# A 31-tap depthwise convolution on TensorE, laid out as two token phases of 64 channels

## What is computed

```python
ga, gg = jnp.split(glu, 2, axis=-1)              # 512 tokens x 512 channels each
u = ga * jax.nn.sigmoid(gg)
u = causal_dwconv(u, conv_b_w, conv_b_b)         # 31 taps, one filter for each channel
b_out = jax.nn.silu(layernorm(u, ln_b_g, ln_b_b))
x = x + jnp.concatenate([a_out, b_out], axis=-1) @ w_out
```

## Time and profile before

| | |
|---|---|
| times of three runs | 2129.69, 2136.82, 2138.82 us; median 2136.82 |
| profiled execution | 2137.5 us: its span, and nothing is shown outside it |
| busy over the span | PE 92%, PEld 75%, DVE 51%, ACT 34%, POOL 49% |
| stage under change (sparse attention) | 204.5 to 318 us |
| matmuls of the convolution | 62 x 3 = 186, with 186 weight loads |

### The profile page before, as it was taken

The page is one execution under the profiler, slowest core; times in us unless marked ns, Lnnn a source line. Parts: engine busy times, 40 slices in busy tenths (PEclk is TensorE's granted clock), DMA queues, the critical chain, the costliest instruction groups (busy, mean ns, idle before and its releaser), DMA issues.

```text
span 2137.5 us, 31171 instructions
## 1 busy us (share of the span) xinstructions
PE 1975.8 (92%) x10443; PEld 1607.7 (75%) x10443; DVE 1098.4 (51%) x1811; ACT 733.2 (34%) x1233; POOL 1046.9 (49%) x576
## 2 busy tenths in 40 slices
PE   7888888979999999778999999999997799999997
PEld 5677666768887888556778888887876678888886
DVE  6777973654677696689333223132128834132232
ACT  4323234344222313435432222233226643222223
POOL 5466426535865644680554444456443244444442
PEclk9999999999999999989999999999999999999999
DMA  4224002323332333100333333334345423333332
GB/s 144 72 86 121 11 15 75 89 50 89 98 98 83 94 99 91 57 2 0 89 91 97 97 100 89 98 97 100 98 114 123 104 69 90 97 98 98 98 89 89
DMA packets 344697, 181.64 MB, mean 85 GB/s; under 512 B 28206, under 2 KB 335782, under 8 KB 344614
## 3 DMA queue, kind: packets, MB, share of 16 engines
q1 hardware_dynamic: 343872, 179.91, 30.1%
q10 hardware_dynamic: 742, 0.68, 0.1%
HBM read 162.73 MB, written 2.10 MB: 77 GB/s over the span
## 4 chain that ended last, share of the span: by engine, by line
PE 51%; issue 13%; DVE 11%; POOL 9%; POOLq 6%; DVEq 4%; ACT 4%; DMA 2%; SPq 0%; ACTq 0%
PE ACC L1464 16%; PE ACC L1465 15%; PE ACC L1470 15%; POOL WL L1128 7%; POOLq L1138 2%; DVE CV L2161 2%; DVE PTL L2261 1%; DVEq L2255 1%; POOLq L1311 1%; POOLq L1323 1%; ACT WH L565 1%; DVEq L2165 1%; DVE NMX L2249 1%; PE O L1586 1%; DVEq L2700 1%
## 5 line engine op out<-in xcount | busy, mean ns | idle before, releaser
L1128 POOL TENSOR_TENSOR WL<-RAW,WH 128x1024 fp32r<-128x1024 f32 (+1 forms) x308 | 733.0, 2382 | 785.2 <-ACT WH L565 717.8
L1464 PE MATMUL ACC<-PH,WH 128*128 128x512 f32 x1248 | 495.8, 397 | 11.9 <-DVE PL L1995 3.6
L1465 PE MATMUL ACC<-PL,WH 128*128 128x512 f32 x1248 | 489.9, 393 | 0.0
L565 ACT ACTIVATE WH<-RAW 128x1024 fp32r<-128x1024 f32 (+1 forms) x308 | 317.6, 1033 | 498.6 <-PE ACC L1470 415.5
L1464 PE MATMUL ACC<-QH,WH 128*128 128x512 f32 (+1 forms) x1136 | 431.1, 384 | 23.1 <-ACT WH L565 17.2
L1465 PE MATMUL ACC<-QL,WH 128*128 128x512 f32 (+1 forms) x1136 | 426.3, 380 | 0.0
L1470 PE MATMUL ACC<-PH,WL 128*128 128x512 f32 x1248 | 311.1, 391 | 0.0
L1464 PEld LDWEIGHTS ACC<-PH,WH 128*128 128x128 f32 x1248 | 236.9, 190 | 71.1 <-DVE PL L1995 4.8
L1470 PE MATMUL ACC<-QH,WL 128*128 128x512 f32 (+1 forms) x1136 | 271.9, 380 | 11.0 <-POOL WL L1128 10.8
L1465 PEld LDWEIGHTS ACC<-PL,WH 128*128 128x128 f32 x1248 | 236.7, 190 | 49.4 <-issue 1.0
L1470 PEld LDWEIGHTS ACC<-PH,WL 128*128 128x128 f32 x1248 | 234.0, 188 | 52.6 <-issue 3.3
(11 more groups left out here) (413 smaller groups left out, 2423.3 us busy)
## 6 DMA issues: line engine op xcount, KB each, us to landing
RAW<-in_mlp_w_dram SPq DMA_DIRECT2D x128, 512.0 KB, 4.1
RAW<-in_w_gate_dram SPq DMA_DIRECT2D x22, 512.0 KB, 3.8
RAW<-in_w_up_dram SPq DMA_DIRECT2D x22, 512.0 KB, 3.7
RAW<-in_w_in_dram SPq DMA_DIRECT2D x16, 512.0 KB, 3.9
RAW<-in_w_down_dram SPq DMA_DIRECT2D x16, 512.0 KB, 4.1
RAW<-in_ssm_w_glu_dram SPq DMA_DIRECT2D x16, 512.0 KB, 3.9
RAW<-in_w_kvf_dram SPq DMA_DIRECT2D x16, 512.0 KB, 3.9
RAW<-in_w_k_cross_dram SPq DMA_DIRECT2D x8, 512.0 KB, 4.1
```

The costliest lines, as they stand in the source:

```text
L565: act.activation(WH[:, s, 0:kc], RAW[:, s, 0:kc], ACT.Copy).then_inc(w_hi, 1)
L1128: pool.tensor_tensor(WL[:, s, 0:kc], RAW[:, s, 0:kc], WH[:, s, 0:kc], ALU.subtract).then_inc(w_lo, 1)
L1464: pe.matmul(ACC[s][:, 0:n], WH[:, s, k, :], xh[:, k, :], start=(k == 0), stop=False)
L1465: pe.matmul(ACC[s][:, 0:n], WH[:, s, k, :], xl[:, k, :], start=False, stop=False)
```

## The change

The 128 channels of a block are treated as two groups g of 64. For a group the partitions 0 to 63 hold the odd tokens and 64 to 127 the even tokens, 256 columns, behind 16 columns of zeros. One 128x128 matrix then carries up to four taps (from either phase to either phase), and a group takes 16 steps of three matmuls with 256 columns: 2 blocks x 2 groups x 16 x 3 = 192 matmuls. The two groups use the two halves of `ST`. For this:

- ScalarE issues four transfers that swap the halves of the tap weights and of the bias (`WSW`, `BSW`) where it rounded the taps before, and arranges and rounds the taps later (`phase_taps`: four small copies, a drain, the rounding), ahead of `rounded(3)`. `WC`, `WCH`, `WCL` are 128 columns wide in place of 124.
- between `memk` and `memv` it makes the phase layout `UP` of each block by four copies of 64x256 with a stride of two tokens, then a drain, and rounds 128x512 in place of 128x542.
- `convolved` is four copies of 64x256 that write every second token.
- GpSimd clears `WC` at the start, makes `EYE2` (two identities of 64 side by side, 128x64), clears the 16 columns ahead of `UH` and `UL`, and multiplies 16 x 64 in place of 8 x 128 columns for a set of matrices.
- the taps are spread over the tiles by the same rule, now 32 steps for a block in place of 31.
- some semaphores are merged (`f_exp`, `f_ln` into `f_soft`; `silu_done` into `branch_hi`) and unused ones dropped; no instruction is added or moved by it.

```diff
+LEAD = 16
+STEPS = 2 * LEAD
...
+        UP = at("UP", [P, 2, 2, T // 2], F32, 147968)
+        UH = at("UH", [P, 2, 2, LEAD + T // 2], F32R, 16384)
+        UL = at("UL", [P, 2, 2, LEAD + T // 2], F32R, 20736)
...
             act.wait_ge(vec_c, 2)
-            act.activation(WCH[:], WC, ACT.Copy).then_inc(wc_hi, 1)
+            bias = COLUMN["conv_b_b"][1]
+            for to, of in ((LOWER, UPPER), (UPPER, LOWER)):
+                act.dma_start(WSW[to, :], VEC[of, 1, 0:BCH * CONVW]).then_inc(vec_in, 16)
+                act.dma_start(BSW[to, :], VEC[of, 0, bias:bias + BCH]).then_inc(vec_in, 16)
+
+            def phase_taps():
+
+                act.wait_ge(vec_in, 16 * (len(VECTORS) + 3))
+                act.wait_ge(u_zero, 1)
+                for g, own_taps, swapped in ((0, LOWER, UPPER), (1, UPPER, LOWER)):
+                    for rows, taps in ((own_taps, VEC[own_taps, 1, 0:BCH * CONVW]), (swapped, WSW[swapped, :])):
+                        late = 1 if rows == UPPER else 0
+                        act.activation(WC[rows, :, g, late:late + CONVW],
+                                       taps.rearrange("p (k c) -> p c k", c=BCH)[:, 2:4, :], ACT.Copy)
+                act.drain()
+                act.activation(WCH[:], WC[:], ACT.Copy).then_inc(wc_hi, 1)
...
             act.activation(MD[:], MV[:], ACT.Sqrt).then_inc(mem_std, 1)
+            phase_taps()
             rounded(3)
...
                 if name == "memk":
+                    act.wait_ge(rope_done, 8)
                     for j in range(2):
                         act.wait_ge(u_ready, 3 + j)
-                        act.activation(UH[:, j, :], U[:, 2 + j, :], ACT.Copy).then_inc(u_hi, 1)
+                        for g, of in enumerate((LOWER, UPPER)):
+                            tokens = U[of, 2 + j, PAD:PAD + T].rearrange("p (m r) -> p r m", r=2)
+                            for r, to in ((1, LOWER), (0, UPPER)):
+                                act.activation(UP[to, j, g, :], tokens[:, r, :], ACT.Copy)
+                        act.drain()
+                        act.activation(UH[:, j, :, LEAD:], UP[:, j], ACT.Copy).then_inc(u_hi, 1)
...
                 act.wait_ge(diag_used, 4 * j + 4)
-                act.activation(CV[2 + j][:], ST[:], ACT.Identity, bias=column("conv_b_b", 2 + j))\
-                   .then_inc(conv_pe, 1)
+                for g, to in enumerate((LOWER, UPPER)):
+                    tokens = CV[2 + j][to, :].rearrange("p (m q) -> p q m", q=2)
+                    for q, of in ((1, LOWER), (0, UPPER)):
+                        bias = column("conv_b_b", 2 + j)[of] if of == to else BSW[of, 2 + j:3 + j]
+                        ins = act.activation(tokens[:, q, :], ST[of, g * T // 2:(g + 1) * T // 2], ACT.Identity, bias=bias)
+                ins.then_inc(conv_pe, 1)
...
+            pool.memset(WC[:], 0.0)
+            pool.drain()
...
-            pool.tensor_tensor(WCL[:], WC, WCH[:], ALU.subtract)
+            pool.tensor_tensor(WCL[:], WC[:], WCH[:], ALU.subtract)
+            pool.tensor_tensor(EYE2[:], IDENT[:, LOWER], IDENT[:, UPPER], ALU.add)
...
             def inputs_low(j):
+                if j == 0:
+                    for x in (UH, UL):
+                        pool.memset(x[:].bitcast(F32)[:, :, :, 0:LEAD], 0.0)
+                    pool.drain()
                 pool.wait_ge(u_hi, j + 1)
-                pool.tensor_tensor(UL[:, j, :], U[:, 2 + j, :], UH[:, j, :], ALU.subtract).then_inc(u_lo, 1)
+                pool.tensor_tensor(UL[:, j, :, LEAD:], UP[:, j], UH[:, j, :, LEAD:], ALU.subtract).then_inc(u_lo, 1)
...
-                    x = slice(k, k + T)
-                    mm = three(ST[:], DGH[j % 2][:, k % TAPS, :], DGL[j % 2][:, k % TAPS, :], UH[:, c, x], UL[:, c, x],
-                               k == 0, k == CONVW - 1)
+                    x = slice(1 + k, 1 + k + T // 2)
+                    mm = three(ST[:, g * T // 2:(g + 1) * T // 2], DGH[j % 2][:, k % TAPS, :], DGL[j % 2][:, k % TAPS, :],
+                               UH[:, c, g, x], UL[:, c, g, x], k == 0, k == LEAD - 1)
```

More of the change, by code:

```diff
@@ L199, in build_program @@
         CV = [at(f"CV{c}", [P, T], F32, (184320, 152576, 34816, 36864)[c]) for c in range(BCH)]
-        UH = at("UH", [P, 2, PAD + T], F32R, 16384)
-        UL = at("UL", [P, 2, PAD + T], F32R, 20736)
+        UP = at("UP", [P, 2, 2, T // 2], F32, 147968)
+        UH = at("UH", [P, 2, 2, LEAD + T // 2], F32R, 16384)
+        UL = at("UL", [P, 2, 2, LEAD + T // 2], F32R, 20736)
         DGH = [at(f"DGH{b}", [P, TAPS, P], F32R, (57344, 73728)[b]) for b in range(2)]
         DGL = [at(f"DGL{b}", [P, TAPS, P], F32R, (61440, 77824)[b]) for b in range(2)]
-        WCH = at("WCH", [P, BCH * CONVW], F32R, 210176)
-        WCL = at("WCL", [P, BCH * CONVW], F32R, 210688)
-        WC = VEC[:, 1, 0:BCH * CONVW]
+        WCH = at("WCH", [P, 2, 2, 2 * LEAD], F32R, 210176)
+        WCL = at("WCL", [P, 2, 2, 2 * LEAD], F32R, 210688)
+        WC = at("WC", [P, 2, 2, 2 * LEAD], F32, 211456)
+        EYE2 = at("EYE2", [P, 64], F32, 211968)
+        WSW = at("WSW", [P, BCH * CONVW], F32, 212224)
+        BSW = at("BSW", [P, BCH], F32, 212736)
+        LOWER, UPPER = slice(0, 64), slice(64, P)
         G = at("G", [P, 2 + T], F32, 155648)
@@ L358, in build_program @@
         rho_used, powers, w_made, c_made, cleared = (sem(n) for n in ("rho_used", "powers", "w_made", "c_made", "cleared"))
-        normed_x, un_ready, uc_ready = sem("normed_x"), sem("un_ready"), sem("uc_ready")
+        un_ready, uc_ready = sem("un_ready"), sem("uc_ready")
         glu_out = sem("glu_out")
         sq2_ready, sq2_used, diag2, bc2 = (sem(n) for n in ("sq2_ready", "sq2_used", "diag2", "bc2"))
-        fw_zero, fw_in, fw_hi, fw_lo, f_mm, f_abs, f_exp, f_ln, f_sum, f_ready = (
-            sem(n) for n in ("fw_zero", "fw_in", "fw_hi", "fw_lo", "f_mm", "f_abs", "f_exp", "f_ln", "f_sum", "f_ready"))
+        fw_zero, fw_in, fw_hi, fw_lo, f_mm, f_abs, f_soft, f_sum, f_ready = (
+            sem(n) for n in ("fw_zero", "fw_in", "fw_hi", "fw_lo", "f_mm", "f_abs", "f_soft", "f_sum", "f_ready"))
         split_hi, split_lo, stacked, bias_in = (
@@ L1072, in _ @@
             act.wait_ge(f_abs, 1)
[L1073 to L1075 removed]
+            act.activation(F[:], F[:], ACT.Exp, scale=-1.0).then_inc(f_soft, 1)
+            act.wait_ge(f_soft, 1)
+            act.activation(F[:], F[:], ACT.Ln, bias=ONES[:, 0:1]).then_inc(f_soft, 1)
             def split_high(c):
@@ L1149, in _ @@
             pool.wait_ge(wc_hi, 1)
-            pool.tensor_tensor(WCL[:], WC, WCH[:], ALU.subtract)
+            pool.tensor_tensor(WCL[:], WC[:], WCH[:], ALU.subtract)
+            pool.tensor_tensor(EYE2[:], IDENT[:, LOWER], IDENT[:, UPPER], ALU.add)
             pool.drain()
             def diagonals(j):
-                c, first = 2 + j // 4, j % 4 * TAPS
-                n = min(TAPS, CONVW - first)
+                c, g, half = j // 4, j // 2 % 2, j % 2
+                n = 2 * TAPS
                 if j >= 2:
@@ L1159, in diagonals @@
                 for to, w in ((DGH, WCH), (DGL, WCL)):
-                    taps = w[:].rearrange("p (k c) -> p k c", c=BCH)[:, first:first + n, c]
-                    ins = pool.tensor_tensor(to[j % 2][:, 0:n, :], IDENT[:, None, :].to_broadcast([P, n, P]),
-                                             taps.bitcast(F32)[:, :, None].to_broadcast([P, n, P]), ALU.mult)
+                    taps = w[:, c, g, half * n:half * n + n]
+                    ins = pool.tensor_tensor(to[j % 2][:].rearrange("p e (q f) -> p (e q) f", q=2),
+                                             EYE2[:, None, :].to_broadcast([P, n, 64]),
+                                             taps.bitcast(F32)[:, :, None].to_broadcast([P, n, 64]), ALU.mult)
                 ins.then_inc(diag_ready, 1)
@@ L1701, in convolve @@
                 for m in range(first, last):
-                    c, k = divmod(m, CONVW)
-                    j = 4 * c + k // TAPS
+                    c, k = divmod(m, STEPS)
+                    g, k = divmod(k, LEAD)
+                    j = 4 * c + 2 * g + k // TAPS
                     if k % TAPS == 0:
                         pe.wait_ge(diag_ready, j + 1)
-                    if k == 0 and c:
+                    if k == 0 and g == 0 and c:
                         pe.wait_ge(conv_pe, c)
-                    x = slice(k, k + T)
-                    mm = three(ST[:], DGH[j % 2][:, k % TAPS, :], DGL[j % 2][:, k % TAPS, :], UH[:, c, x], UL[:, c, x],
-                               k == 0, k == CONVW - 1)
-                    if k % TAPS == TAPS - 1 or k == CONVW - 1:
+                    x = slice(1 + k, 1 + k + T // 2)
+                    mm = three(ST[:, g * T // 2:(g + 1) * T // 2], DGH[j % 2][:, k % TAPS, :], DGL[j % 2][:, k % TAPS, :],
+                               UH[:, c, g, x], UL[:, c, g, x], k == 0, k == LEAD - 1)
+                    if k % TAPS == TAPS - 1:
                         mm.then_inc(diag_used, 1)
```

(6 more changed lines are left out.)

18 lines of the change are left out of this document (7 added, 11 removed).

## The result

| | median of the runs | lowest to highest | profiled span |
|---|---|---|---|
| before | 2135.19 us (20 runs) | 2129.69 to 2141.07 | 2137.5 |
| after | 2138.89 us (20 runs) | 2135.10 to 2142.89 | 2139.4 |

The account below looks back on a forecast made before the run. VectorE was taken to bound the sparse attention, the only stage with the convolution. TensorE -2.0, copies +1.9, start +0.5 and accumulator copies +0.2 sum to +0.6: 2138.1 on the span, 2137.4 beside the median, range 2130.5 to 2145.

Parts of the forecast that it names:

- TensorE's part, -2.0: Sparse attention: shorter products cut VectorE's three waits for ScalarE's rounded tile from 2.4 to about 0.4 us; range 0 to -3.4.
- VectorE's pace, as forecast: Sparse attention: VectorE, not TensorE, sets the pace; it stays as busy, and TensorE waits more for it in each tile.
- The rival of stalls that shift: Sparse stage: GpSimd's matrices slow VectorE's taps at other moments; a third less of 11 us excess gives 2133.5; chance 0.10.
- The copies, +1.9: Between `memk` and `memv`: ScalarE's eight copies delay the second `memv` rounding, so attention starts 1.9 us later.
- that chain has nothing spare: From the late `memv` rounding through GpSimd's remainders and SyncE's loads to the first score matmul: the delay passes on whole.
- The start, +0.5: Kernel start: ScalarE's four transfers delay the rounding of block 1 that TensorE wants, 0.5 us; ends 0 and +1.2.
- the thin cover of the square root: Kernel start: square root some 1.5 us late, its result wanted only after TensorE's sixteen matmuls; prices the +1.2 end.
- ScalarE's second set of copies, +0.2: Tile 23: four copies out of the accumulator in place of one hold up ScalarE's next exponential; +0.2 us, 0 to 0.8.
- Dear copies: Between `memk` and `memv`: strided copies cost 4.5 us in place of 1.9, giving 2140.0, or 2142.5; chance 0.10.
- The clock: Sparse stage: idler TensorE drops to half clock; six two-tile stretches and the channel sum give 2152; chance 0.08.
- 256 columns not faster: Convolution products: a weight load of 0.19 us sets the pace, so little comes back and the time is 2139; chance 0.04.
- The signs that were named: Profile after: expected product steps, waits, rounding, load and first-score times; stage clock under 0.9 or lower mean tap would refute.

Follow-up runs that it names:

- before + copies: Kernel before plus the eight copies and two drains between `memk` and `memv`, their result unused: 2137.27 us, ratio 1.0015.
- before + transfers: Kernel before plus the four transfers that swap the tap weights and bias at the start, their result unused: 2135.91 us, ratio 1.0002.
- before, 256 columns: Kernel before with its 186 convolution matmuls cut to the first 256 columns, nothing else changed: 2132.99 us, ratio 0.9992.
- after, moved: Kernel after with ScalarE's transfers put behind block 3's rounding, first copies ahead of `memk`'s end, second behind the first `memv` block: 2136.25 us, ratio 1.0009.
- the kernel before with early taps: Kernel before with 13 in place of 8 of VectorE's taps done ahead of the sparse stage: 2134.93 us, ratio 1.0008.
- the first group of experiments: Kernel before with 256 columns, copies or transfers, and kernel after with ScalarE's work moved: 2132.99, 2137.27, 2135.91, 2136.25 us.
- a stage with VectorE relieved: Block 1 of the convolution left out from tap 8 on (23 VectorE taps), in kernel before and kernel after: 2120.59 and 2122.57 us.

## Why the prediction was right, and which terms were off

The moments that the profiles of the kernels that compute everything show, in us. The stage is from the start of VectorE's first reduction to the end of its last tap; the third column is the way from the first tap to that reduction.

| kernel | first tap at | first tap to first reduction | stage |
|---|---|---|---|
| before | 169.05 | 36.0 | 86.3 |
| before + copies | 168.01 | 38.4 | 84.9 |
| before + transfers | 170.44 | 36.4 | 84.7 |
| before, 256 columns | 168.50 | 36.2 | 83.5 |
| after | 169.83 | 37.8 | 85.3 |
| after, moved | 169.74 | 35.8 | 85.0 |

(The line with 256 columns leaves half of each product out, as its expectation says.)

**TensorE's part, -2.0: the term that was mis-sized.** The three kernels whose stage is that of before have 86.3, 84.9 and 84.7 us. The profile that the prediction rested on shows the longest, with 2.4 us of waits for the rounded tile at 250 us; the other two have these waits too:

```profile
DVE PTL L2269 <- ACT PTH L720: 1.0, 2, 0.8
```
```profile
DVE PTL L2268 <- ACT PTH L719: 0.9, 2, 0.7
```

The term took the gain from one execution's stretch at half clock. In that stretch it had tile 12 right (1.9 us), and was wrong on tile 13 (0.2 for one us, as the clock came back later) and on the copies ahead (1.3 for 0.7), as the chains above show: 0.8 us in place of 2.0. The three kernels with 256 columns have 83.5, 85.3 and 85.0 us, on average 0.7 less than the three with 512 (84.6 against 85.3). So what it is worth is between 0 and 1, with the two whole layouts at 0. By themselves, without the copies out of the accumulator, the products give 1.8 (85.3 to 83.5), and the runs of that kernel agree (-1.7, from -3.6 to +0.4). Two things work against them. The copies ahead of tile 12 start 0.49 us apart and were priced at 0.32. And the clock falls more often: over 204.5 to 293 us it is 0.92 after and 0.96 before, 0.90 in the kernel before with 256 columns and 0.87 in the kernel after with moved work. The range's own end of 0 for this term was the right one.

**VectorE's pace, as forecast.** It is busy for 79.1 us of 88.5 against 80.9, less by the later start, and TensorE waits longer for it (20.6 us for 9.1). The rival of stalls that shift did come about, and is nil in its sum. The 46 taps fell from 43.8 to 40.8 us of busy time. Of the divisions beside them those of 128x384 rose from 3.8 to 5.8 and those of 128x256 from 2.1 to 4.1, while those of 128x512 got shorter, from a mean of 904 ns to one of 735. Against their lengths without GpSimd's products (747 ns a tap; 486, 420, 354 and 287 ns a division) taps and divisions of the stage are 11.3 + 5.0 = 16.3 us too long before and 8.4 + 7.7 = 16.1 after, an estimate from these rows. GpSimd's matrices fall on other instructions, and the total stays.

**The copies, +1.9: right in the sum, by two errors.** They took 4.7 us and not 3.9, and the rounding of the second `memv` block started at 176.33, not near 174.8. But "that chain has nothing spare" was wrong too: 3.5 us late at 176.33 (0.7 of it from the start) are 2.6 late at the first score. By the way from first tap to first reduction the price is 1.8 after and 2.4 with the copies alone, 2.1 by all profiles; that it came out at the forecast 1.9 is luck, since a cost too low met a slack taken as none. Moving the copies takes the price away in one profile and not in another.

**The start, +0.5: 0.9, within its ends.** The price can be read at TensorE's second unit. In the eight profiles with neither the transfers at the start nor a half clock there it starts 2.64 to 2.67 us after the first of the eight matmuls ahead of it; in the two with the transfers alone it starts 3.54 after, having waited 0.77 for ScalarE. That is +0.9, where 0.5 was taken and 1.2 was the upper end. The eight matmuls from 25.5 us on ran at half clock in the profile after, and in three other kernels, among them the kernel before with early taps, which has no transfers:

```profile
25.46 3.36 PE L1510 MATMUL ACC<-PH,WL 128*128 128x512 f32 x8
```
```profile
25.75 3.62 PE L1470 MATMUL ACC<-PH,WL 128*128 128x512 f32 x8
```

There the second unit starts 4.0 us after, where two with the half clock and no transfers have 3.7 and 4.6; what the transfers add in that case can't be told. The first tap says no more: 168.6 us on average in the eight (167.8 to 169.8), 169.86 and 170.44 with the transfers alone, 169.74 and 170.77 with the half clock alone, 169.83 and 169.89 with both. From the second unit to the first tap there are 141.1 us in both with the transfers alone and 140.2 to 141.7 in the eight, so nothing shows that the thin cover of the square root failed. The runs of the kernel with transfers alone, +0.4 (-1.7 to +2.8), hold 0 and 0.9 alike. Why some executions start at half clock was not tested.

**ScalarE's second set of copies, +0.2: nil where it can be seen.** From the end of the last tap to the centring of the branch there are 8.56 to 8.58 us in the kernel before, in the one after and in all four kernels of the first group of experiments.

**The sum.** About +0.9 for the start, +2 for the copies, 0 for the stage: +3, where 3.7 to 4.1 was measured (2.6 to 5.6). The parts measured alone give -1.7 + 3.2 + 0.4 = +1.9, each within 2 us or so. The last microsecond is not placed: it is below what single profiles tell. At the centring of the branch the profile after is 1.6 us behind (301.5 against 299.9). In the unchanged code behind it single profiles differ by more than the whole effect: from the product with `RS` at about 330 us to the last reduction of scores at about 1718 they take 1383.2 to 1389.9 us, without an order by version (1387.6 before, 1389.9 after), and from 304 to 316 us the granted clock is 0.72 in the profile before and 1.00 in the one after.

**The rivals.** Dear copies: dearer by 0.8 us, absorbed again. The clock: it fell in three places of the stage and took part of the gain back (some 0.8 us in tile 13). No run shows the six stretches of two tiles, with 1 us of wait in each tile, that its 12 us count: VectorE's waits for the rounded tile are 1.6 us in all. 256 columns not faster: excluded, since the products start 0.12 us apart at full clock against 0.233 for 512 columns, and a stage with VectorE relieved is 3.2 us shorter. Its number, 2139, came nearest to the measured one all the same, which shows that a right time does not prove a mechanism.

**The signs that were named.** The load of `outa` (201.61 for 201.5) and the first score (207.06 for 206.9) held, as did TensorE's longer waits for VectorE. VectorE's single waits were to stay under 0.7 and reached 0.8 and 1.3. The rounding was 1.5 us off; its 174.8 had left out the start's 0.5 that it was said to hold. A granted clock under 0.9 over the stage, or a drop in the mean tap, was to prove the forecast wrong: the clock was 0.92, the mean tap dropped from 992 to 929 ns. By that second sign the forecast would be wrong. It was badly chosen, since the divisions took up what the taps lost.

## What to carry to other kernels

Before an engine's saved work is booked as time, look at who sets the pace in that very stage; here TensorE was 92% busy over the whole and gave 1.8 us of the stage when its products were halved, nothing clear of noise once ScalarE's extra copies were paid, while moving the matrices from GpSimd to ScalarE in the old layout gave 6.8 us. A stall that one profile shows at one place, above all behind a fall of the clock, is one draw: look at a second execution before a term rests on it. A layout that halves columns but doubles the number of small copies is paid for on ScalarE, at nearly the price of whole ones (0.49 us from start to start for 64x256 out of the accumulator, against 0.59 on the chain for one of 128x512).

## What the runs showed of the hardware that was not expected

- Four ScalarE copies of 64x256 with a stride of two between halves of the partitions start 0.45 us apart at 0.43 us each, and those out of the accumulator with a bias 0.49 apart at 0.48: no overlap. Copies of 64x512 and 64x640 in the kernel before, each within one half of the partitions, do not overlap either. Copies of 128x128 with a scale do (0.39 long, 0.29 apart). So neither the accumulator nor a copy from one half to the other is needed for it; half the partitions and strides were not tried apart.
- GpSimd's products beside VectorE's taps cost 12 us of an 85 us stage (16 in the new layout), and the loss can move from taps (43.8 to 40.8 us) to divisions of one input (up by 4 us in two shapes, while a third got shorter) with the sum of both as it was, 16 us.
- TensorE's clock was at 1.2 GHz for eight dense matmuls at 25.5 us in four of fourteen profiles, with and without changes near that place, and at 2.4 GHz in the others.
